# Conformer convolution on one core: shifted copies by way of DRAM in five transfers a tile, and layer-norm sums added on GpSimd about a provisional mean

## The chip, the cores and the metric

The program runs on one core of one Trainium2 chip. The metric is the device time of one launch in microseconds (us). PE is TensorE's matmul, PEld its weight load, DVE VectorE, ACT ScalarE, POOL GpSimd, SP SyncE, which issues nearly all transfers here; SPq is its DMA issue. Line numbers (L242) are those of the kernel before.

## The reference, cut to what matters

Two layers of a conformer step over 512 prompt tokens and 8 sample tokens, 1024 features wide. Layer 0 mixes with attention, layer 1 with this convolution module; each layer has two feed-forward halves and an embedding step around it.

```
def conv_module(h, buf, w_in, w_dw, b_dw, ln_g, ln_b, w_out):
    u = h @ w_in
    g = u[..., :D_MODEL] * jax.nn.sigmoid(u[..., D_MODEL:])
    xc = jnp.concatenate([buf.astype(g.dtype), g], axis=1)
    y = lax.conv_general_dilated(xc, w_dw[:, None, :], window_strides=(1,), padding='VALID', ...,
                                 feature_group_count=D_MODEL) + b_dw          # 31 taps, one filter a feature
    y = jax.nn.silu(layernorm(y, ln_g, ln_b))
    return y @ w_out, xc[:, -(CONV_WIDTH - 1):]
def layernorm(x, g, b):
    mu = jnp.mean(xf, axis=-1, keepdims=True)
    var = jnp.mean(jnp.square(xf - mu), axis=-1, keepdims=True)
    y = (xf - mu) * lax.rsqrt(var + LN_EPS) * g + b
```

## The kernel before, in words

Activations lie with features on the 128 partitions (eight feature tiles, k = 0 to 7) and the 520 tokens along the free axis, in PSUM as two halves of 260. Every large product is three matmuls: weights and activations are split into a high part and a rest (`w_hi`, `w_lo`, `h_hi`, `h_lo`), and `products` (L242) runs hi*hi, hi*lo and lo*hi. A weight slab of 128 x 1024 is fetched by SP into `w_raw` (`load_slab`, L221), split by ACT (L227) and DVE (L231), and used by PE. The order on each engine is the order in which the code is written; semaphores alone join the engines.

The stage that the change touches is the convolution of layer 1, in the functions `conv_sp`, `conv_pe`, `conv_act`, `conv_dve` and `conv_pool`. For each feature tile k:

- PE makes the two halves of `w_in` (`tile(k, 0)` and `tile(k, 1)`, 48 matmuls each). DVE brings them out of PSUM (`scaled`, L293), ACT takes the sigmoid (L1700), DVE multiplies them (`gated`, L1766) into `g_pad`, which holds 30 zeros ahead of 512 tokens in two buffers.
- Of the 31 taps, 28 go to PE. For these `g4` holds four copies of the tile, each shifted by j = 0 to 3 tokens, on 32 partitions per shift, with the features in four groups of 32. SP makes them in `shifted(k)` with 16 transfers from SBUF to SBUF (L1505), one for each shift and group. PE then runs `taps_pe(k)` (L1556): 28 matmuls (56 in the trace) with `diag4`, the taps spread over small diagonals, which POOL makes (L1847) from `tap4`, the taps in the same arrangement. `tap4` is filled by another 16 transfers (L1517) from `taps_j`.
- The last 3 taps are DVE's (`own_taps`, L1777 and L1781). `finish(k)` (L1789 to L1795) adds both parts into y. It runs one tile later than the tile's products.
- For the layer norm PE sums y over features by matmuls with ones (`ln_sum`, L1564), tile by tile, two tiles behind, into one PSUM slot. After the last tile DVE subtracts the mean from each of the eight tiles (L1823), ACT squares each (L1718), and PE sums each square with ones (L1602); ACT makes 1/sqrt (L1723, L1725); DVE scales (L1827), ACT applies Silu (L1728) and makes `c_hi`, DVE makes `c_lo` (L1834), and only then can the products with `w_out` begin (`conv_out_pe`).

PE's written order is tile(0,0), tile(0,1), tile(1,0), 16 transposes of the convolution's state, tile(1,1), taps 0, and from k = 2 on tile(k,0), tile(k,1), taps k-1, `ln_sum(k-2)`. After the loop come eight small transposes (L1594), `ln_sum(6)`, taps 7, `ln_sum(7)` and the sums of squares. SP's written order puts the transfers for `tap4` ahead of `shifted(0)`, and the slabs of tile b+3 ahead of `shifted(b+1)`.

Of the kernel before, what the change touches and what calls it, by code (L numbers as in the profile page):

```python
# [48 lines left out]
def build(nc, io):  # L49
# [4 lines left out]
    with ctx:  # L54
# [54 lines left out]
        conv_kept = (("g_last", [P, KD, PAD + NS], F32), ("y", [P, KD, T], F32), ("cv_tok", [PAD + NS, D], F32))  # L109
        g_last, y, cv_tok, ident4, taps_j, tap4, g_pad, g4, diag4, own_a, own_b, st_rows, st = phase_memory(  # L110
            *conv_kept, ("ident4", [P, Q], F32), ("taps_j", [P, 4, KD, GROUPS], F32), ("tap4", [P, 4, KD, GROUPS], F32),
            ("g_pad", [P, 2, PAD + TP], F32), ("g4", [P, 2, 4, GW], F32), ("diag4", [P, KD, 4, GROUPS, Q], F32),
# [372 lines left out]
        def load_sp(sp):  # L485
# [24 lines left out]
        def load_pool(pool):  # L510
# [979 lines left out]
        def conv_sp(sp):  # L1490
# [23 lines left out]
            sp.wait_ge(taps_j_ok, 1)  # L1514
            for j in range(4):
                for g in range(4):
                    sp.dma_start(tap4[j * Q:(j + 1) * Q, g, :, :], taps_j[g * Q:(g + 1) * Q, j, :, :]).then_inc(tap4_in, 16)  # L1517
            shifted(0)
# [17 lines left out]
        def conv_pe(pe):  # L1536
# [9 lines left out]
            def taps_pe(k):  # L1546

                pe.wait_ge(g4_in[k % 2], 256 * (k // 2 + 1))
                pe.wait_ge(diag4_ok, k + 1)
                if k < 2:  # L1550
                    pe.wait_ge(state_ok, 3)
                else:
                    pe.wait_ge(y_ok, k - 1)
                for i in range(GROUPS):
                    for g in range(4):
                        ins = pe.matmul(ps[g * Q:(g + 1) * Q, 3, k % 2, :], diag4[:, k, g, i, :],  # L1556
                                        g4[:, k % 2, g, 4 * i:4 * i + TP], start=i == 0, stop=i == GROUPS - 1)
                ins.then_inc(taps_mm, 1)

            def ln_sum(k):  # L1560

                pe.wait_ge(y_ok, k + 1)
                for b in range(2):
                    ins = pe.matmul(slot(2)[:, b, :], ones[:, :], y[:, k, b * HALF:(b + 1) * HALF],  # L1564
                                    start=k == 0, stop=k == KD - 1)
                return ins

# [27 lines left out]
            ins.then_inc(tail_mm, 1)  # L1595
            ln_sum(KD - 2)
            taps_pe(KD - 1)
            ln_sum(KD - 1).then_inc(ln_mm, 1)
            for k in range(KD):
                pe.wait_ge(ysq_ok, k + 1)  # L1600
                for b in range(2):
                    ins = pe.matmul(slot(1)[:, b, :], ones[:, :], square[:, k % 2, b * HALF:(b + 1) * HALF],  # L1602
                                    start=k == 0, stop=k == KD - 1)
                ins.then_inc(ln_mm, 1)

# [58 lines left out]
        def conv_out_dve(dve):  # L1664
# [22 lines left out]
            for m in range(6, KD):  # L1687
                split_lo(dve, n0 + m, m % 2)
                add(m - 2)
                x_post_dve(dve, CO, 1, 2, m - 2)  # L1690

        def conv_act(act, prev):
            n0 = C["slab"]
# [8 lines left out]
            for j in range(2):  # L1702
                split_hi(act, n0 + 2 + j, n0 // 2 + 1, j)
                if j == 0:
                    stat_act(act, C)
            sigmoid(0)
            for k in range(1, KD):
                if k < KD - 1:
                    for j in range(2):
                        split_hi(act, n0 + 2 * k + 2 + j, n0 // 2 + k + 1, j)  # L1710
                sigmoid(k)
            for j in range(2):
                split_hi(act, CO["slab"] + j, CO["slab"] // 2, j)
            for k in range(KD):
                act.wait_ge(yc_ok, k + 1)
                if k >= 2:
                    act.wait_ge(ln_mm, k)
                act.activation(square[:, k % 2, :], y[:, k, :], ACT.Square).then_inc(ysq_ok, 1)  # L1718
# [3 lines left out]
            act.wait_ge(ln_mm, KD + 1)  # L1722
            act.activation(halves(s_gate[:, :]), slot(1), ACT.Ln, scale=1.0 / D, bias=eps[:, 1:2]).then_inc(var_ok, 1)  # L1723
            act.wait_ge(var_ok, 1)
# [8 lines left out]
        def conv_dve(dve, prev_evac, prev_lo):  # L1733
# [69 lines left out]
            for k in range(1, KD):  # L1803
# [9 lines left out]
                if k == 1:  # L1813
                    state_sum()
                finish(k - 1)
            own_taps(KD - 1)
            finish(KD - 1)
            for j in range(2):
                split_lo(dve, CO["slab"] + j, j)
            for k in range(KD):  # L1820
                dve.wait_ge(ln_mm, 1)
                yk = halves(y[:, k, :])
                dve.scalar_tensor_tensor(yk, slot(2), 1.0 / D, yk, ALU.mult, ALU.subtract).then_inc(yc_ok, 1)  # L1823
            dve.wait_ge(var_ok, 2)
            for k in range(KD):
                dve.wait_ge(ysq_ok, k + 1)
                dve.scalar_tensor_tensor(y[:, k, :], y[:, k, :], -1.0, s_up[:, :], ALU.mult, ALU.mult).then_inc(yn_ok, 1)  # L1827
# [8 lines left out]
        def conv_pool(pool):  # L1836
            pool.tensor_copy(taps_j[:, :, :, :], taps[:, 0:TAPS_PE * KD].rearrange(
                "p (i j k) -> p j k i", i=GROUPS, j=4)).then_inc(taps_j_ok, 1)
            pool.wait_ge(state_ok, 3)
# [3 lines left out]

            pool.wait_ge(tap4_in, 256)
            pool.wait_ge(ident4_ok, 1)
            for k in range(KD):
                pool.tensor_tensor(diag4[:, k, :, :, :], ident4[:, :].unsqueeze(1).unsqueeze(1).broadcast_to([P, 4, GROUPS, Q]),  # L1847
                                   tap4[:, :, k, :].unsqueeze(3).broadcast_to([P, 4, GROUPS, Q]), ALU.mult).then_inc(diag4_ok, 1)


# [299 lines left out]
```

## Time and profile before

| | |
|---|---|
| median of 3 runs | 2306.94 us (2306.43 to 2313.22) |
| the profiled execution | 2307.65 us, its span 2305.8 us |
| PE busy | 2212.5 us, 96% of the span |
| DVE, ACT, POOL busy | 1086.1, 752.1 and 130.8 us |
| chain that ended last | PE 85%, of which L242 80% of the span; SPq 2% on L1505 |
| convolution stage | from about 1602 to 1800 us of the span |

The slice view (40 slices of 57.6 us) has PE at nine tenths or more nearly throughout; three of the four slices that hold the convolution have 7, 8 and 8. PE bounds the kernel, so what counts are the places where it stands still, and the work that it is given.

### The profile page before, as it was taken

The page shows a single profiled execution, that of the slowest core. Times are in us where ns is not written, and L with a number is a line of the kernel's source. Part 1 is how long each engine was busy: PE and PEld are TensorE (multiplying, and loading weights), DVE is VectorE, ACT ScalarE, POOL GpSimd, SP SyncE. Part 2 cuts the span into 40 slices and gives each one's busy share as a digit, 9 for nine tenths or more (in the row PEclk, how much of TensorE's full clock was granted, in tenths as well). Part 3 has the DMA queues.
Part 4 walks back from the last instruction along what each step waited for, and adds up shares of the span by engine and source line. Part 5 has one row for each costly group of instructions (what it writes and reads, how often), then busy time and mean ns, then how long its engine had stood idle before and what let it go on. Part 6 is the DMA issues. An engine that isn't in the chain of part 4 may idle for free.

```text
span 2305.8 us, 43575 instructions
## 1 busy us (share of the span) xinstructions
PE 2212.5 (96%) x18009; PEld 2111.0 (92%) x18009; DVE 1086.1 (47%) x1269; ACT 752.1 (33%) x1011; POOL 130.8 (6%) x101
## 2 busy tenths in 40 slices
PE   7999999979998999999999999999798899999998
PEld 7999999967777999999999999999575899999998
DVE  5444433378884444443354444433633444443344
ACT  4222222446663322222244222222111532222223
POOL 2000001010000100000010000001300100000100
PEclk9999999989998999999999999999898999999999
DMA  3333332435673333333232333323443233333322
GB/s 113 91 91 91 105 88 83 153 94 187 220 239 106 101 91 91 91 99 97 68 101 83 91 91 91 103 88 91 109 129 82 58 92 91 91 91 100 94 71 83
DMA packets 380347, 237.98 MB, mean 103 GB/s; under 512 B 10090, under 2 KB 363850, under 8 KB 380264
## 3 DMA queue, kind: packets, MB, share of 16 engines
q1 hardware_dynamic: 371560, 232.56, 33.9%
q10 hardware_dynamic: 8704, 4.26, 0.6%
q8 instruction: 59, 0.97, 0.2%
q14 instruction: 24, 0.20, 0.0%
HBM read 220.36 MB, written 7.53 MB: 99 GB/s over the span
## 4 chain that ended last, share of the span: by engine, by line
PE 85%; DVE 6%; issue 3%; SPq 2%; ACT 2%; DMA 1%; ACTq 0%; DVEq 0%
PE ps L242 80%; SPq L1505 2%; PE ps L1556 2%; DVE sg_m L1325 1%; DVE kc L1341 1%; DVE w_lo L231 1%; DVE sg_p L1332 1%; PE ps L1891 1%; ACT w_hi L227 0%; SPq L1517 0%; DVE h_lo L259 0%; PE ps L809 0%; DMA g<-g_pad 0%; DMA xs_tok<-in_x_sample 0%; PE ps L1602 0%
## 5 line engine op out<-in xcount | busy, mean ns | idle before, releaser
L242 PE MATMUL ps<-h_hi,w_hi 128*128 128x260 f32 x3712 | 757.9, 285 | 13.6 <-DVE w_lo L231 9.0
L242 PE MATMUL ps<-h_hi,w_lo 128*128 128x260 f32 x3712 | 749.8, 284 | 0.0
L242 PE MATMUL ps<-h_lo,w_hi 128*128 128x260 f32 x3712 | 748.6, 283 | 0.0
L227 ACT ACTIVATE w_hi<-w_raw 128x1024 fp32r<-128x1024 f32 (+1 forms) x314 | 353.9, 1127 | 1140.4 <-PE ps L242 1098.3
L242 PEld LDWEIGHTS ps<-h_hi,w_hi 128*128 128x128 f32 x3712 | 575.5, 189 | 22.3 <-DVE w_lo L231 10.9
L242 PEld LDWEIGHTS ps<-h_hi,w_lo 128*128 128x128 f32 x3712 | 574.0, 189 | 0.0
L242 PEld LDWEIGHTS ps<-h_lo,w_hi 128*128 128x128 f32 x3712 | 573.1, 189 | 0.0
L231 DVE TENSOR_TENSOR w_lo<-w_raw,w_hi 128x1024 fp32r<-128x1024 f32 (+1 forms) x316 | 420.0, 1329 | 270.4 <-ACT w_hi L227 270.0
L242 PE MATMUL ps<-a_hi,w_hi 128*128 128x260 f32 x1408 | 283.9, 283 | 0.0
L242 PE MATMUL ps<-a_hi,w_lo 128*128 128x260 f32 x1408 | 283.2, 282 | 0.0
L242 PE MATMUL ps<-a_lo,w_hi 128*128 128x260 f32 x1408 | 282.7, 282 | 0.0
L293 DVE TENSOR_TENSOR s_up<-ps,rms 128x520 f32<-128x520 f32 x108 | 75.6, 700 | 338.3 <-PE ps L242 332.1
L242 PEld LDWEIGHTS ps<-a_lo,w_hi 128*128 128x128 f32 x1408 | 217.3, 188 | 0.0
L242 PEld LDWEIGHTS ps<-a_hi,w_hi 128*128 128x128 f32 x1408 | 216.7, 188 | 0.0
L242 PEld LDWEIGHTS ps<-a_hi,w_lo 128*128 128x128 f32 x1408 | 216.6, 188 | 0.0
L293 DVE TENSOR_TENSOR s_gate<-ps,rms 128x520 f32<-128x520 f32 x116 | 81.2, 700 | 189.0 <-PE ps L242 149.3
L299 DVE SCALAR_TENSOR_TENSOR x<-ps,x 128x520 f32 (+1 forms) x42 | 29.4, 700 | 199.0 <-PE ps L242 199.0
L272 POOL TENSOR_TENSOR sumsq<-sumsq,square 128x520 f32<-128x520 f32 x56 | 87.4, 1561 | 480.4 <-ACT square L255 450.1
L317 ACT ACTIVATE a_hi<-s_prod 128x520 f32 (+1 forms) x88 | 56.2, 639 | 176.2 <-DVE s_prod L324 176.2
L326 DVE TENSOR_TENSOR a_lo<-s_prod,a_hi 128x520 f32 (+1 forms) x88 | 61.6, 700 | 80.7 <-ACT a_hi L317 80.7
L269 POOL COPY sumsq<-square 128x520 f32<-128x520 f32 x8 | 6.7, 840 | 1534.9 <-ACT square L255 1511.2
L259 DVE SCALAR_TENSOR_TENSOR h_lo<-x,gains,h_hi 128x520 fp32r<-128x520 f32 (+1 forms) x64 | 80.6, 1267 | 3.4 <-ACT h_hi L253 2.0
(215 smaller groups left out, 1562.4 us busy)
## 6 DMA issues: line engine op xcount, KB each, us to landing
w_raw<-in_ffn_wg SPq DMA_DIRECT2D x88, 512.0 KB, 3.8
w_raw<-in_ffn_wu SPq DMA_DIRECT2D x88, 512.0 KB, 3.8
w_raw<-in_ffn_wd SPq DMA_DIRECT2D x64, 704.0 KB, 4.4
kc<-in_cache_k SPq DMA_DIRECT2D x32, 512.0 KB, 5.5
vc<-in_cache_v SPq DMA_DIRECT2D x28, 512.0 KB, 5.9
w_raw<-in_attn_w_qkv SPq DMA_DIRECT2D x24, 512.0 KB, 4.5
g<-g_pad SPq DMA_DIRECT2D x128, 67.0 KB, 2.1
w_raw<-in_ple_w_gate SPq DMA_DIRECT2D x16, 512.0 KB, 3.7
```

What stands on the lines that cost most here:

```text
L227: act.activation(w_hi[:, j, 0:cols], w_raw[:, j, 0:cols], ACT.Copy).then_inc(slab_hi, 1)
L231: dve.tensor_tensor(w_lo[:, j, 0:cols], w_raw[:, j, 0:cols], w_hi[:, j, 0:cols].bitcast(F32), ALU.subtract).then_inc(slab_lo, 1)
L242: ins = pe.matmul(out[:, b_, :], a[:, j, w], b[:, k0 + k, b_ * HALF:(b_ + 1) * HALF], start=(first and k == kts[0] and n == 0), stop=(last ...
L259: dve.scalar_tensor_tensor(h_lo[:, ds(m, 1), :].rearrange("p a t -> p (a t)"), x[:, ds(m, 1), :].rearrange("p a t -> p (a t)"), gain_col(l ...
L272: pool.tensor_tensor(sumsq[:, :], sumsq[:, :], square[:, m2, :], ALU.add).then_inc(acc_ok, 1)
L293: dve.tensor_tensor(halves(out), slot(s), halves(rms[:, :]), ALU.mult).then_inc(evac, 1)
L299: dve.scalar_tensor_tensor(xm, slot(s), factor, xm, ALU.mult, ALU.add).then_inc(evac, 1)
L317: act.activation(a_hi[:, ds(f, 1), :].rearrange("p a t -> p (a t)"), s_prod[:, :], ACT.Copy).then_inc(a_hi_ok, 1)
L326: dve.tensor_tensor(a_lo[:, ds(f, 1), :].rearrange("p a t -> p (a t)"), s_prod[:, :], a_hi[:, ds(f, 1), :].rearrange("p a t -> p (a t)").b ...
L1325: ins = dve.tensor_tensor_scan(m, m, zero[:, :].broadcast_to([P, (i + 1) * P]), 1.0, ALU.mult, ALU.max)
L1505: sp.dma_start(g4[j * Q:(j + 1) * Q, k % 2, g, :], g_pad[g * Q:(g + 1) * Q, k % 2, j:j + GW]).then_inc(g4_in[k % 2], 16)
L1556: ins = pe.matmul(ps[g * Q:(g + 1) * Q, 3, k % 2, :], diag4[:, k, g, i, :], g4[:, k % 2, g, 4 * i:4 * i + TP], start=i == 0, stop=i == GRO ...
```

## The change

Four parts.

1. `shifted(k)`: one transfer writes `g_pad` to a DRAM buffer `g_rows` (128 rows of 542 values), SP waits until it has landed, and four transfers (one a shift, 32 partitions x 4 groups x 536 values) read it into `g4`. `gated(k)` now waits for the write of tile k-2 and no longer for its shifted copies.
2. `taps_j` is made by POOL at the start of the program, in memory of the loading phase, and written to a DRAM buffer `taps_rows` by SP; four transfers fill `tap4` from there, ahead of the state's load. POOL's part before `diag4` is now only the product for the state.
3. The sum of y is formed by POOL, tile by tile, in `y_sum` (the memory of `sumsq`), and PE sums it over features twice: after four tiles (`across`, within k = 5) and after eight. Twice the first sum over 1024 is `mean_4`, a provisional mean.
4. DVE takes each tile's deviation from `mean_4` (`deviation`), ACT squares it, POOL adds the squares in `d_sum` (the memory of `log_ms`); tiles 0 to 6 within the loop by the table `DEVS`, tile 7 at the end. PE sums `d_sum` once. The variance is that sum over 1024 less the square of (true mean - `mean_4`). The eight `ln_sum` and the eight sums of squares on PE are gone. DVE's two splits of the first `w_out` slabs now stand before `finish(7)`, and y is centred behind the sums.

```
-        g_last, y, cv_tok, ident4, taps_j, tap4, ... = phase_memory(
+        g_last, y, cv_tok, ident4, mean_4, tap4, ... = phase_memory(
...
+        taps_rows = nc.dram_tensor("taps_rows", (P, 4 * KD * GROUPS), F32, kind="Internal").ap()
+        g_rows = nc.dram_tensor("g_rows", (2, P, PAD + TP), F32, kind="Internal").ap()
+        y_sum, d_sum, dev = sumsq, log_ms, s_prod
...                                                     (load_sp, its end)
+            sp.wait_ge(taps_j_ok, 1)
+            sp.dma_start(taps_rows[:, :], taps_j[:, :, :, :].rearrange("p j k i -> p (j k i)")).then_inc(taps_rows_in, 16)
...                                                     (load_pool, its end; was the start of conv_pool)
+            pool.wait_ge(vec_ok, 2)
+            pool.tensor_copy(taps_j[:, :, :, :], taps[:, 0:TAPS_PE * KD].rearrange(
+                "p (i j k) -> p j k i", i=GROUPS, j=4)).then_inc(taps_j_ok, 1)
...                                                     (shifted, in conv_sp)
+                sp.dma_start(g_rows[k % 2], g_pad[:, k % 2, :]).then_inc(g_rows_in, 16)
+                sp.wait_ge(g_rows_in, 16 * k + 16)
                 for j in range(4):
-                    for g in range(4):
-                        sp.dma_start(g4[j * Q:(j + 1) * Q, k % 2, g, :],
-                                     g_pad[g * Q:(g + 1) * Q, k % 2, j:j + GW]).then_inc(g4_in[k % 2], 16)
+                    sp.dma_start(g4[j * Q:(j + 1) * Q, k % 2, :, :],
+                                 g_rows[k % 2].rearrange("(g c) t -> c g t", g=4)[:, :, j:j + GW]).then_inc(g4_in[k % 2], 16)
...                                                     (conv_sp; the tap4 loop after both(2) is gone)
+            sp.wait_ge(taps_rows_in, 16)
+            for j in range(4):
+                sp.dma_start(tap4[j * Q:(j + 1) * Q, :, :, :].rearrange("p g k i -> p g (k i)"),
+                             taps_rows.rearrange("(g c) (j r) -> j c g r", g=4, j=4)[j]).then_inc(tap4_in, 16)
...                                                     (conv_pe)
-            def ln_sum(k):
...
+            def across(s, src):
                 for b in range(2):
+                    ins = pe.matmul(slot(s)[:, b, :], ones[:, :], src[:, b * HALF:(b + 1) * HALF], start=True, stop=True)
+                ins.then_inc(ln_mm, 1)
...
                 tile(k, 1)
+                if k == 5:
+                    pe.wait_ge(y_sum_ok, 4)
+                    across(2, y_sum)
                 taps_pe(k - 1)
-                ln_sum(k - 2)
...
-            ln_sum(KD - 2)
             taps_pe(KD - 1)
-            ln_sum(KD - 1).then_inc(ln_mm, 1)
-            for k in range(KD):
-                pe.wait_ge(ysq_ok, k + 1)
...
+            pe.wait_ge(mean_4_ok, 1)
+            pe.wait_ge(y_sum_ok, KD)
+            across(2, y_sum)
+            pe.wait_ge(d_sum_ok, KD)
+            across(1, d_sum)
...
+        DEVS = {k: {5: (0, 1), 6: (2, 3, 4), 7: (5, 6)}.get(k, ()) for k in range(KD)}
...                                                     (conv_act)
+            def squared(k):
+                act.wait_ge(dev_ok, k + 1)
+                if k >= 2:
+                    act.wait_ge(d_sum_ok, k - 1)
+                act.activation(square[:, k % 2, :], dev[:, :], ACT.Square).then_inc(ysq_ok, 1)
...
+            act.wait_ge(off_ok, 1)
+            act.activation(s_act[:, :], dev[:, :], ACT.Square).then_inc(off_ok, 1)
+            act.wait_ge(off_ok, 3)
+            act.activation(s_gate[:, :], s_gate[:, :], ACT.Ln, bias=eps[:, 1:2]).then_inc(var_ok, 1)
...                                                     (conv_dve)
-                    dve.wait_ge(g4_in[k % 2], 256 * (k // 2))
+                    dve.wait_ge(g_rows_in, 16 * (k - 1))
...
+            def deviation(k):
+                dve.wait_ge(mean_4_ok, 1)
+                dve.wait_ge(y_ok, k + 1)
+                if k:
+                    dve.wait_ge(ysq_ok, k)
+                dve.tensor_tensor(dev[:, :], y[:, k, :], mean_4[:, :], ALU.subtract).then_inc(dev_ok, 1)
...
             own_taps(KD - 1)
-            finish(KD - 1)
             for j in range(2):
                 split_lo(dve, CO["slab"] + j, j)
+            finish(KD - 1)
+            deviation(KD - 1)
+            dve.wait_ge(ln_mm, 2)
+            dve.wait_ge(ysq_ok, KD)
+            dve.scalar_tensor_tensor(halves(dev[:, :]), slot(2), 1.0 / D, halves(mean_4[:, :]),
+                                     ALU.mult, ALU.subtract).then_inc(off_ok, 1)
...
+            centred(0)
+            centred(1)
+            dve.wait_ge(ln_mm, 3)
+            dve.wait_ge(off_ok, 2)
+            dve.scalar_tensor_tensor(halves(s_gate[:, :]), slot(1), 1.0 / D, halves(s_act[:, :]),
+                                     ALU.mult, ALU.subtract).then_inc(off_ok, 1)
+            for k in range(2, KD):
+                centred(k)
...                                                     (conv_sums_pool, new, run behind conv_pool)
+            for k in range(5):
+                add_y(k)
+            for k in range(5, KD):
+                for d in DEVS[k]:
+                    add_d(d)
+                add_y(k)
+            add_d(KD - 1)
```

`add_y(k)` waits for y of tile k and adds it to `y_sum` (the fifth also waits until PE has read the first sum); `add_d(k)` waits for the square and adds it to `d_sum`; the first of each is a copy.

**The order on SP**, from the last slabs ahead of the convolution to the shifted copies of tile 1. Before:

```order
L1511 DMA st_rows<-in_state_conv 120x2x1024
L221 DMA w_raw<-in_conv_w_in 128x8x128 x2
L1517 DMA tap<-taps_j 32x56 x16
L1505 DMA g<-g_pad 32x536 x16
L221 DMA w_raw<-in_conv_w_in 128x8x128 x2
L1525 DMA out_new_conv_sample<-st_rows 29x2x1024
L1505 DMA g<-g_pad 32x536 x16
```

Of the change, whose line numbers are its own:

```order
L1530 DMA tap<-taps_rows 32x4x56 x4
L1532 DMA st_rows<-in_state_conv 120x2x1024
L232 DMA w_raw<-in_conv_w_in 128x8x128 x2
L1519 DMA g_rows<-g_pad 128x542
L1522 DMA g<-g_rows 32x4x536 x4
L232 DMA w_raw<-in_conv_w_in 128x8x128 x2
L1542 DMA out_new_conv_sample<-st_rows 29x2x1024
L1519 DMA g_rows<-g_pad 128x542
L1522 DMA g<-g_rows 32x4x536 x4
```

Sixteen small transfers have gone from ahead of the first shifted copies, four stand ahead of the state's load, and each group of sixteen has become one and four.

**The order on DVE**, from the last of DVE's own taps on. Before:

```order
L1781 SCALAR_TENSOR_TENSOR own_a<-g_pad,taps,own_a 128x512
L1789 TENSOR_TENSOR own_b<-own_b,ps 128x512
L1792 SCALAR_TENSOR_TENSOR y<-g_last,taps,y 128x8
L1795 TENSOR_TENSOR y<-own_a,own_b 128x512
L231 TENSOR_TENSOR w_lo<-w_raw,w_hi 128x1024 x2
L1823 SCALAR_TENSOR_TENSOR y<-ps,y 128x520 x8
L1827 SCALAR_TENSOR_TENSOR y<-y,s_up 128x520 x2
```

Of the change (`s_prod` is the memory of `dev`, `mean` is `mean_4`):

```order
L1810 SCALAR_TENSOR_TENSOR own_a<-g_pad,taps,own_a 128x512
L242 TENSOR_TENSOR w_lo<-w_raw,w_hi 128x1024 x2
L1818 TENSOR_TENSOR own_b<-own_b,ps 128x512
L1821 SCALAR_TENSOR_TENSOR y<-g_last,taps,y 128x8
L1824 TENSOR_TENSOR y<-own_a,own_b 128x512
L1796 TENSOR_TENSOR s_prod<-y,mean 128x520
L1857 SCALAR_TENSOR_TENSOR s_prod<-ps,mean 128x520
L1864 SCALAR_TENSOR_TENSOR y<-ps,y 128x520 x2
L1870 SCALAR_TENSOR_TENSOR s_gate<-ps,s_act 128x520
L1864 SCALAR_TENSOR_TENSOR y<-ps,y 128x520 x6
L1877 SCALAR_TENSOR_TENSOR y<-y,s_up 128x520 x2
```

The two weight splits have moved ahead of the end of y, and three instructions have come in behind it.

**The order on POOL**, behind the state's product, of the change (before, only the product and the eight `diag` stood here):

```order
L1888 TENSOR_TENSOR st<-st,taps 128x1920
L1895 TENSOR_TENSOR diag<-ident,tap 128x896 x8
L1904 COPY sumsq<-y 128x520
L1909 TENSOR_TENSOR sumsq<-sumsq,y 128x520 x4
L1915 COPY log_ms<-square 128x520
L1918 TENSOR_TENSOR log_ms<-log_ms,square 128x520
L1909 TENSOR_TENSOR sumsq<-sumsq,y 128x520
L1918 TENSOR_TENSOR log_ms<-log_ms,square 128x520 x3
L1909 TENSOR_TENSOR sumsq<-sumsq,y 128x520
L1918 TENSOR_TENSOR log_ms<-log_ms,square 128x520 x2
```

One more addition of each kind follows. Sixteen instructions of 128 x 520 have come to POOL.

## Rows read from the trace of the kernel before

**Rows 1.** Waits between 1600 and 1900 us: in total, times, longest.

```profile
PE ps L1556 <- DMA g<-g_pad: 18.7, 4, 11.8
```

**Rows 2.** The chain that ended last, 1590 to 1880 us: start, duration, what.

```profile
1617.33 0.91 SPq L1517
...
1680.26 6.22 PE ps L1556 x56
...
1780.11 2.27 DVE w_lo L231 x2
...
1797.46 0.83 ACT y L1728
1798.31 0.65 ACT c_hi L1731
1798.98 0.71 DVE c_lo L1834
...
1799.83 54.61 PE ps L242 x432
```

**Rows 3.** PE in order of time, in brackets idle time ahead and its releaser.

```profile
1639.42 9.10 PE L1556 MATMUL ps<-g,diag 128*32 128x512 f32 x56 [11.76 <-DMA g<-g_pad]
...
1660.16 6.22 PE L1556 MATMUL ps<-g,diag 128*32 128x512 f32 x56
1666.30 1.14 PE L1564 MATMUL ps<-y,ones 128*128 128x260 f32 x4
...
1769.88 8.73 PE L1556 MATMUL ps<-g,diag 128*32 128x512 f32 x56 [4.74 <-DMA g<-g_pad]
```

**Rows 4.** Windows: engines' busy time, PEclk, DMA share, GB/s.

```profile
1636.00:1637.00 1.00, 0.00 (x0) 0.00 (x0) 1.00 (x2) 0.53 (x1) 1.00 (x1) 0.50 0.59 137
...
1772.00:1773.00 1.00, 1.00 (x8) 0.20 (x4) 0.00 (x0) 0.13 (x1) 0.00 (x0) 0.50 1.01 391
...
1799.83:1805.50 5.67, 5.67 (x26) 5.67 (x27) 5.17 (x9) 5.54 (x9) 0.00 (x0) 0.50 0.00 0
```

**Rows 5.** SP's issues in order of time, convolution stage.

```profile
1617.33 10.43 SPq L1517 DMA_DIRECT2D tap<-taps_j  x16
...
1758.32 10.02 SPq L1505 DMA_DIRECT2D g<-g_pad  x16
```

**Rows 6.** DMA issues by kind: count, KB each, median us to landing.

```profile
g<-g_pad SPq DMA_DIRECT2D x128, 67.0 KB, 2.1
...
out_y_prompt<-out_tok SPq DMA_DIRECT2D x8, 256.0 KB, 2.2
```

**Rows 7.** POOL: two rows in order of time, one group of the page.

```profile
1623.54 5.41 POOL L1840 TENSOR_TENSOR st<-st,taps 128x1920 f32<-128x1920 f32 x1 [16.61 <-DVE st L1748]
1628.96 16.48 POOL L1847 TENSOR_TENSOR diag<-ident,tap 128x896 f32<-128x896 f32 x8
...
L272 POOL TENSOR_TENSOR sumsq<-sumsq,square 128x520 f32<-128x520 f32 x56 | 87.4, 1561 | 480.4 <-ACT square L255 450.1
```

**Rows 8.** DVE in order of time.

```profile
1617.62 0.69 DVE L1766 TENSOR_TENSOR g_pad<-s_up,s_act 128x512 f32<-128x512 f32 x1 [0.72 <-ACT s_act L1700]
...
1623.99 6.05 DVE L231 TENSOR_TENSOR w_lo<-w_raw,w_hi 128x1024 fp32r<-128x1024 f32 x1
...
1638.38 2.18 DVE L1766 TENSOR_TENSOR g_pad<-s_up,s_act 128x512 f32<-128x512 f32 x1
...
1750.50 0.70 DVE L293 TENSOR_TENSOR s_up<-ps,rms 128x520 f32<-128x520 f32 x1 [5.41 <-PE ps L242]
...
1782.30 4.94 DVE L1823 SCALAR_TENSOR_TENSOR y<-ps,y 128x520 f32<-128x520 f32 x8
...
1796.18 1.31 DVE L1827 SCALAR_TENSOR_TENSOR y<-y,s_up 128x520 f32<-128x520 f32 x2 [8.95 <-ACT s_up L1725]
```

**Rows 9.** The start of the program, POOL and SP in order of time.

```profile
14.61 0.70 POOL L269 COPY sumsq<-square 128x520 f32<-128x520 f32 x1 [9.98 <-ACT square L255]
...
21.98 0.42 SPq L221 DMA_DIRECT2D w_raw<-in_ffn_wg  x1
```

More of the change, by code:

```diff
@@ L109, in build @@
         conv_kept = (("g_last", [P, KD, PAD + NS], F32), ("y", [P, KD, T], F32), ("cv_tok", [PAD + NS, D], F32))
-        g_last, y, cv_tok, ident4, taps_j, tap4, g_pad, g4, diag4, own_a, own_b, st_rows, st = phase_memory(
-            *conv_kept, ("ident4", [P, Q], F32), ("taps_j", [P, 4, KD, GROUPS], F32), ("tap4", [P, 4, KD, GROUPS], F32),
+        g_last, y, cv_tok, ident4, mean_4, tap4, g_pad, g4, diag4, own_a, own_b, st_rows, st = phase_memory(
+            *conv_kept, ("ident4", [P, Q], F32), ("mean_4", [P, T], F32), ("tap4", [P, 4, KD, GROUPS], F32),
             ("g_pad", [P, 2, PAD + TP], F32), ("g4", [P, 2, 4, GW], F32), ("diag4", [P, KD, 4, GROUPS, Q], F32),
@@ L172, in build @@
         taps_j_ok = sem("taps_j_ok")
+        taps_rows_in = sem("taps_rows_in")
+        g_rows_in = sem("g_rows_in")
+        y_sum_ok = sem("y_sum_ok")
+        d_sum_ok = sem("d_sum_ok")
+        dev_ok = sem("dev_ok")
+        mean_4_ok = sem("mean_4_ok")
+        off_ok = sem("off_ok")
         tap4_in = sem("tap4_in")
@@ L1513, in conv_sp @@
             both(2)
[L1514 to L1517, printed above, removed]
             shifted(0)
@@ L1546, in taps_pe @@
             def taps_pe(k):
-                pe.wait_ge(g4_in[k % 2], 256 * (k // 2 + 1))
+                pe.wait_ge(g4_in[k % 2], 64 * (k // 2 + 1))
                 pe.wait_ge(diag4_ok, k + 1)
@@ L1595, in conv_pe @@
             ins.then_inc(tail_mm, 1)
-            ln_sum(KD - 2)
             taps_pe(KD - 1)
-            ln_sum(KD - 1).then_inc(ln_mm, 1)
-            for k in range(KD):
-                pe.wait_ge(ysq_ok, k + 1)
[L1601 to L1604, printed above, removed]
+            pe.wait_ge(mean_4_ok, 1)
[3 more added lines that the diff above has]
+            across(1, d_sum)
         CO = at["mixout", 1]
@@ L1711, in conv_act @@
                 sigmoid(k)
+                for d in DEVS[k]:
+                    squared(d)
             for j in range(2):
                 split_hi(act, CO["slab"] + j, CO["slab"] // 2, j)
[L1714 to L1718, printed above, removed]
+            squared(KD - 1)
             act.wait_ge(tail_mm, 1)
@@ L1815, in conv_dve, with centred @@
                 finish(k - 1)
+                if k == 5:
+                    dve.wait_ge(ln_mm, 1)
+                    dve.tensor_scalar(halves(mean_4[:, :]), slot(2), 2.0 / D, None, ALU.mult).then_inc(mean_4_ok, 1)
+                for d in DEVS[k]:
+                    deviation(d)
             own_taps(KD - 1)
-            finish(KD - 1)
             for j in range(2):
                 split_lo(dve, CO["slab"] + j, j)
-            for k in range(KD):
-                dve.wait_ge(ln_mm, 1)
+            finish(KD - 1)
[4 more added lines that the diff above has]
+                                     ALU.mult, ALU.subtract).then_inc(off_ok, 1)
+            def centred(k):
+                dve.wait_ge(dev_ok, k + 1)
+                dve.wait_ge(y_sum_ok, k + 1)
                 yk = halves(y[:, k, :])
                 dve.scalar_tensor_tensor(yk, slot(2), 1.0 / D, yk, ALU.mult, ALU.subtract).then_inc(yc_ok, 1)
+            centred(0)
[6 more added lines that the diff above has]
+                centred(k)
             dve.wait_ge(var_ok, 2)
             for k in range(KD):
-                dve.wait_ge(ysq_ok, k + 1)
+                dve.wait_ge(yc_ok, k + 1)
                 dve.scalar_tensor_tensor(y[:, k, :], y[:, k, :], -1.0, s_up[:, :], ALU.mult, ALU.mult).then_inc(yn_ok, 1)
@@ L1842, in conv_pool @@
                                    [P, KD, NS, PAD]), ALU.mult).then_inc(st_prod, 1)
-            pool.wait_ge(tap4_in, 256)
+            pool.wait_ge(tap4_in, 64)
             pool.wait_ge(ident4_ok, 1)
@@ L1848, in conv_pool, with conv_sums_pool, add_y, add_d @@
                                    tap4[:, :, k, :].unsqueeze(3).broadcast_to([P, 4, GROUPS, Q]), ALU.mult).then_inc(diag4_ok, 1)
+        def conv_sums_pool(pool):
+            def add_y(k):
+                pool.wait_ge(y_ok, k + 1)
+                if k == 0:
+                    pool.wait_ge(stat_mm, C["norm"] + 1)
+                    pool.tensor_copy(y_sum[:, :], y[:, 0, :]).then_inc(y_sum_ok, 1)
+                else:
+                    pool.wait_ge(y_sum_ok, k)
+                    if k == 4:
+                        pool.wait_ge(ln_mm, 1)
+                    pool.tensor_tensor(y_sum[:, :], y_sum[:, :], y[:, k, :], ALU.add).then_inc(y_sum_ok, 1)
+            def add_d(k):
+                pool.wait_ge(ysq_ok, k + 1)
+                if k == 0:
+                    pool.wait_ge(rms_ok, C["norm"] + 1)
+                    pool.tensor_copy(d_sum[:, :], square[:, 0, :]).then_inc(d_sum_ok, 1)
+                else:
+                    pool.wait_ge(d_sum_ok, k)
+                    pool.tensor_tensor(d_sum[:, :], d_sum[:, :], square[:, k % 2, :], ALU.add).then_inc(d_sum_ok, 1)
+            for k in range(5):
+                add_y(k)
+            for k in range(5, KD):
+                for d in DEVS[k]:
+                    add_d(d)
+                add_y(k)
+            add_d(KD - 1)
         y_mm = sem("y_mm")
@@ L2059, in _ @@
                 (attn_pool, conv_pool)[layer](pool)
+                if layer == 1:
+                    conv_sums_pool(pool)
                 add_squares_pool(pool, at["mixout", layer])
```

13 lines of the change are left out of this document (3 added, 10 removed).

## The prediction

> **What bounds the kernel now.** The page's busy shares come first: PE is busy 96% of the span and the chain runs 85% through it, so only time in which PE stands still in the convolution stage, or work that it no longer gets, can move the end. The waits view of that stage names the largest stall: PE waited four times for the shifted copies, 18.7 us in all, 11.8 of them once [rows 1]. PE in order of time places them [rows 3]: 11.76 us ahead of taps 0 and 4.74 ahead of taps 7, so 2.2 us are left for the other two. The reader should then look at what PE does next. Taps 0 and taps 7 took 9.10 and 8.73 us, taps 1, without a gap, 6.22 [rows 3], and taps 2, behind one of the small gaps, 6.22 too [rows 2]: after both long gaps the granted clock was at its lower level, as it also was when the products with `w_out` began (0.50 in the 5.67 us from 1799.83) [rows 4]. The chain [rows 2] shows what lay under the first gap: not the copy itself, but SP, busy from 1617.33 with the 16 transfers for `tap4` (10.43 us) before it came to the copies of tile 0 [rows 5]. It shows a third place: y of the last tile is written at 1780.11, and the products with `w_out` begin at 1799.83 [rows 2]. These 19.7 us are the layer norm, one pass behind another.
>
> The sum is made against the profiled execution, 2307.65 us, which lies 0.7 above the median 2306.94; the terms are taken over unchanged. About 0.3% (7 us) is what a measurement can tell from no change here.
>
> **Price of a transfer.** A small copy of 67 KB lands 2.1 us after its issue [rows 6]. While only such copies ran, the DMA engines moved 137 GB/s at a busy share of 0.59 [rows 4], 232 at full share. So of the 2.1 us some 0.3 is the data and 1.8 is fixed. The write of `g_rows` has 277 KB: 1.8 + 1.2 = 3.0 us by this, and 2.2 by the nearest row, the output's 256 KB to DRAM [rows 6]; I take 2.2 and keep 3.0. The four reads have 1.1 MB together: 1.8 + 4.7 = 6.5 us from first issue to last landing. If they ran at the fastest rate seen (391 GB/s, `w_out` slabs over 128 partitions) [rows 4] it would be 4.6. I take 6.5, since the reads fill the same 32 partitions with rows of the same length as the copies that gave 232. So the chain from `g_pad` to taps is 2.2 + 6.5 and 0.2 for two handovers, 8.9 us, against some 10.0 of issuing and 2.1 of landing now [rows 5, 6].
>
> The Trainium skill (SBUF — State Buffer, section "Door 1: The DMA port swizzle") says that 32 partitions reach only half of the ports and end at about 218 GB/s. That speaks against the fast end, and the rate scaled from the row, 232, is near it. By the fit of the page DMA: Bandwidth & Descriptors (section "Anatomy of one DMA"), 2.0 us and bytes at 436 GB/s, the whole chain would be 7.4 us, and the sum below would gain 1.5 us more.
>
> **1. First gap.** With `tap4` filled long before, SP comes to tile 0 as soon as `g_pad` is there, at 1618.3 [rows 8]. A weight slab is in flight ahead of the write (a delay of up to 2 us); the copies land by 1618.4 + 3.0 + 2 + 6.5 = 1629.9 at the latest. Next to be late is POOL: the state's product ends at 1628.95 and the first of eight `diag` takes 16.48 / 8 = 2.06 us [rows 7]. Taps 0 can start at 1631.2 in place of 1639.42: **-8.2 us**. PE still stands for 3.5 us, so I leave taps 0 at the 9.1 us it took. It couldn't use a faster one: `g_pad` of tile 1 is written slowly, at 1640.5 (2.18 us beside POOL) [rows 8], its copies land at about 1640.6 + 2.5 (slab and state rows ahead in the queue) + 2.2 + 6.5 = 1651.8, and PE arrives there at 1631.2 + 9.1 + 11.6 (the two halves between taps 0 and taps 1 [rows 3]) = 1651.9. A gain in clock would be lost in that wait; a slower chain costs here at once. Bounds 5 and 10.
>
> **2. PE's work inside the loop.** Each `ln_sum` is 1.14 us as a group, 1.07 apart [rows 3]. Five (tiles 0 to 4) stand where PE is the bound and go; those of tiles 5 and 6 stand in the gap ahead of taps 7 and give nothing; one `across` comes in at k = 5. 5 x 1.07 - 1.07 = **-4.3 us**. The sum it waits for was finished by POOL some 8 us before.
>
> **3. The two small waits** of 2.2 us together [rows 1, 3]. The copies are wanted some 16 us after `g_pad` and were late because their issue crawled behind slabs; the new chain needs 8.9 and up to 4 for the slab ahead of it: **-2.2 us**, bounds 0 and 2.2.
>
> **4. Last gap.** `g_pad` of tile 7 is there when SP issues at 1758.32 [rows 5]. Taps 7 can start at 1758.4 + 8.9 = 1767.3, against 1769.88: **-2.6 us**. PE has lost two `ln_sum` in this gap, so it stands for 4.74 + 2 x 1.07 - 2.6 = 4.3 us. The gap of 4.74 cost the clock, the two small ones did not [rows 2, 3]; 4.3 is nearer to the former, so taps 7 stays at 8.7. Bounds 0 and, with fast reads and the clock held, 4.5 + 2.5 = 7.
>
> **5. The tail.** From y's last write to the first `w_out` product, the longest path is now: POOL's addition of tile 7, 1.56 [rows 7]; `across`, 1.1 [rows 3]; on DVE the offset, 0.6, eight centrings, 4.94 [rows 8], the variance, 0.7, and one scaling, 0.65 [rows 8]; then Silu 0.83, `c_hi` 0.65, `c_lo` 0.71 [rows 2]; handovers 0.6. Sum 12.3 us against 19.7: **-7.4 us**. The other branch (deviation, square, POOL's second addition, `across`, variance, Ln, Exp) ends near 6.9 us, while DVE still centres until 9.3, so it is covered by 2.4 us. The lower clock at the start of the `w_out` products [rows 4] stays, since PE stands for over 7 us there. The splits of the `w_out` slabs now stand ahead of `finish(7)`; their slabs are issued at about 1764 and are split by 1773, taps 7 ends at 1776. Bounds 4 and 9.
>
> **6. What costs nothing.** POOL's copy of the taps runs at about 13.5 us, before its first addition at 14.61, and SP's write then stands in a wait that lasts until 21.98 [rows 9]. Of the new work, 7 deviations on DVE and 7 squares on ACT lie in the loop, where DVE stands idle 5.4 us before each tile's first half is done [rows 8]; the densest place (tile 6: `finish`, three deviations that wait for squares) needs about 5.0. Without that cover each us over it delays the bringing out of a half, which matters only after another 5 us or so.
>
> Sum: 8.2 + 4.3 + 2.2 + 2.6 + 7.4 = 24.7 us. 2307.65 - 24.7 = 2283.0, and 2282.2 on the median.
>
> **Rivals.**
> (A) *Reads at full rate.* If the reads from DRAM move as the slabs do, taps 7 starts at 1765.4, the gap is 2.4 us, and the clock may hold: 1.9 + 2.5 more, 2278. For it: 391 GB/s was seen. Against: not into 32 partitions. Chance 0.2.
> (B) *DVE and POOL in each other's way.* The split that began at 1623.99 took 6.05 us, against 1.14 for one of the two at 1780.11, and ended 1.1 us after POOL's product did [rows 2, 7, 8]. So DVE stood until POOL was through. In the tail, the deviation and POOL's addition start together; 0.7 us more if DVE goes first. In tile 6 and 7, ten additions of 1.56 us stand beside DVE's deviations, own taps and splits; if every second of them blocks DVE, `g_pad` of tile 7 comes about 3 us late and `finish(7)` 1 to 2 us: about 5 us back, 2287. Against: all of it together fits into the tile's 18 us. Chance 0.15. The Trainium skill (SBUF — State Buffer, section "Who interferes with whom") has the rule: an instruction of VectorE with two SBUF inputs and one of GpSimd that reads SBUF exclude each other for their whole length; by that rule this is the full block that the row shows, and the centrings, which read PSUM, are free of it.
> (C) *The way through DRAM is the new bound.* SP itself waits for the write, with the reads and the slabs of the next tiles queued behind it. In the loop taps k is wanted about 15.5 us after `g_pad`(k), and 3 to 4 of these go to the slab ahead, so it decides once write and reads take over 12 us. For a result slower than before by 7 us, the six tiles in the loop and the last must give back 32 us: 2.7 us of gap and 2.6 of slow clock at each of six, that is write and reads in 15 us, 2314 or more. For it: a write is now ahead of every read and no row here shows that pair back to back. Against: 2.2 us for 256 KB to DRAM. Chance 0.03.
> (D) *The gain is mostly given back*: chain at 12 us, first gap only moved to taps 1 with a second cold start, tail held by the statistics: 2300 to 2310. Chance 0.05.
>
> **Numbers.** My forecast 0.57, A 0.2, B 0.15, D 0.05, C 0.03. The bounds of the five terms, not all at one end, give 15 to 33 us off; with A and B inside, the range is 2274 to 2292. Faster by over 0.3% is everything but C and about half of D, 0.94; within 0.3%, 0.04; slower 0.02.
>
> **What would show it.** Taps 0 starting near 1631 with POOL's `diag` as releaser, and a wait of under 1 us ahead of taps 1; no wait of PE for the copies of tiles 2 to 6; taps 7 about 11 us after the end of `tile(7,1)` (1756.1 before, 1740 or so now) and still near 8.7 us; 12 us between y's last write and the first `w_out` product, with DVE busy in most of it. I am wrong on the transfers if PE waits for copies within the loop, on the tail if DVE's scaling waits for Exp, and on POOL if DVE's own taps or splits take over 2 us there.

## The result and the profile after

| | before | changed |
|---|---|---|
| median of 13 runs each | 2308.3 us | 2304.4 us |
| ratio, 95% interval | | 0.9979 (0.9971 to 0.9988) |
| profiled span | 2305.8 us | 2305.1 us |
| stage, from the norm's sum (L278, now L289) to the first `w_out` product | 191.97 us | 187.66 us |

The change gains about 4 us; 24.7 had been forecast. The two profiled spans differ by only 0.7 us because the changed kernel's stage happened to begin 3.7 us later in its run. Single runs of either kernel scatter by 9 to 10 us from the lowest to the highest, so I compare stages within a trace and medians of runs. One run of one experiment (the transfers alone, 3088.81 us at a granted clock of 0.65 against 0.98 in its others) was in a slower state and is left out of that experiment's numbers. Line numbers below are those of the kernel shown.

The waits view of the changed kernel, 1590 to 1900 us (total, times, longest), answers to [rows 1]:

```profile
PE ps L1573 <- DMA g<-g_rows: 17.5, 3, 7.7
```

The same view for SP:

```profile
SPq L1522 <- DMA g_rows<-g_pad: 57.9, 8, 12.1
```

PE still waits 17.5 us for copies, nearly as long as before. SP waits 7.2 us on average for a write that I had priced at 2.2, because it now has to see each write land before it may issue the reads. PE in order of time, answering to [rows 3]:

```profile
1635.44 8.72 PE L1573 MATMUL ps<-g,diag 128*32 128x512 f32 x56 [4.07 <-issue]
...
1663.57 8.32 PE L1573 MATMUL ps<-g,diag 128*32 128x512 f32 x56 [7.70 <-DMA g<-g_rows]
1683.69 6.22 PE L1573 MATMUL ps<-g,diag 128*32 128x512 f32 x56
1706.78 8.89 PE L1573 MATMUL ps<-g,diag 128*32 128x512 f32 x56 [5.14 <-DMA g<-g_rows]
...
1775.72 8.56 PE L1573 MATMUL ps<-g,diag 128*32 128x512 f32 x56 [4.61 <-DMA g<-g_rows]
1787.28 2.05 PE L1579 MATMUL ps<-sumsq,ones 128*128 128x260 f32 x4 [3.01 <-POOL sumsq L1909]
```

The first gap did shrink, from 11.76 to 4.07 us. But two new ones have opened, ahead of taps 1 and taps 3, and both were followed by the low clock (8.3 and 8.9 us against 6.22). SP's issues show what stood behind them, in answer to [rows 5]:

```profile
1642.67 0.44 SPq L1542 DMA_DIRECT2D out_new_conv_sample<-st_rows  x1
1644.35 0.34 SPq L1519 DMA_DIRECT2D g_rows<-g_pad  x1
1656.25 1.75 SPq L1522 DMA_DIRECT2D g<-g_rows  x4
...
1730.42 0.41 SPq L1519 DMA_DIRECT2D g_rows<-g_pad  x1
1734.75 1.75 SPq L1522 DMA_DIRECT2D g<-g_rows  x4
...
1749.14 0.34 SPq L1519 DMA_DIRECT2D g_rows<-g_pad  x1
1751.56 1.73 SPq L1522 DMA_DIRECT2D g<-g_rows  x4
```

The time from a write to the reads behind it is the write's landing. It was 11.9 us where a store of the sample's state rows (L1542) had been issued just ahead (tile 1), 4.3 behind two weight slabs (tile 5), and 2.4 with nothing ahead (tile 6). All four tiles with a store ahead (1 to 4) read 11.9 to 13.3. The windows of the first of them (columns as in [rows 4]):

```profile
1645.00:1646.00 1.00, 1.00 (x11) 1.00 (x10) 1.00 (x2) 0.00 (x0) 1.00 (x2) 1.00 0.97 342
1647.00:1656.00 9.00, 8.86 (x74) 8.65 (x73) 7.07 (x11) 1.10 (x2) 2.85 (x3) 1.00 0.07 27
1659.00:1663.00 4.00, 0.00 (x0) 0.00 (x0) 0.00 (x0) 0.00 (x0) 0.00 (x0) 0.75 1.07 203
```

The slabs are through by 1646. Then, for nine microseconds, the DMA share is 0.07, about one engine of sixteen, and 27 GB/s flow: 9 x 27 is 243 KB, close to the 232 KB of the store. So I read it like this: the store has 29 rows and runs on one DMA engine, a sixteenth of the write goes to that engine too, and SP waits for it. The experiments below test this reading. The last row shows the reads with slabs among them: all engines busy, 203 GB/s.

### The profile page after: what moved, and what is told of

The parts are those of the page before. It is cut to its first block, busy times and chain, and to the rows that moved or that the text cites. A ratio compares the mean times of both kernels' runs of the same rounds, so it can differ in the third digit from the quotient of the medians.

```text
span 2305.1 us, 43436 instructions
## 1 busy us (share of the span) xinstructions
PE 2207.5 (96%) x17957; PEld 2105.6 (91%) x17957; DVE 1099.3 (48%) x1280; ACT 752.8 (33%) x1012; POOL 152.4 (7%) x117
## 4 chain that ended last, share of the span: by engine, by line
PE 83%; DVE 7%; issue 4%; DMA 3%; ACT 2%; POOL 1%; ACTq 0%; SPq 0%; DVEq 0%; POOLq 0%
PE ps L253 79%; DVE sg_m L1341 1%; DMA g_rows<-g_pad 1%; DVE kc L1357 1%; PE ps L1573 1%; DVE w_lo L242 1%; PE ps L1969 1%; DVE sg_p L1348 1%; DVE zs L1362 1%; DMA g<-g_rows 1%; POOL log_ms L1918 0%; PE ps L825 0%; DMA w_raw<-in_attn_w_qkv 0%; ACT w_hi L238 0%; DVE h_lo L270 0%
```

## The experiments

Theory S: the store's single engine holds up the write. Rival W: a write to DRAM is slow under the slabs' traffic. Rival P: the loss lies in the sums, where POOL holds up DVE.

### Without the stores

```
-                sp.dma_start(out[b, 0:PAD - 1, :, :], rows).then_inc(conv_out, 16)
...
-            sp.wait_ge(conv_out, 96)
+            sp.wait_ge(conv_out, 32)
```

> The changed kernel with the four stores of 29 kept state rows left out (those rows of new_conv_sample are not written). Theory S: each store of 232 KB runs on one of the 16 DMA engines (share 0.06 to 0.07 for some 9 us behind the slabs), and the write of g_rows, one sixteenth of which goes to the same engine, lands 12 us after its issue in place of 2 to 3. Then all eight writes land in 2 to 5 us, PE's waits ahead of taps 1 and taps 3 (7.7 and 5.1 us, and 4.8 of low clock behind them) go, and the time is 2287, 17 to 18 under the change. Rival W: a write to DRAM under the slabs' traffic is slow by itself. Then the four writes of tiles 1 to 4 still land in 8 us or more and the time stays at 2300 to 2305.

2284.5 us, ratio 0.9900 (0.9882 to 0.9918). The eight writes land in 2.2 to 4.9 us with the slabs still ahead of them, and the waits ahead of taps 1 and 3 are gone. W falls.

### The stores moved behind the copies

```
                 both(b + 3)
-                sp.dma_start(out[b, 0:PAD - 1, :, :], rows).then_inc(conv_out, 16)
                 shifted(b + 1)
+                sp.dma_start(out[b, 0:PAD - 1, :, :], rows).then_inc(conv_out, 16)
```

> The changed kernel with each of the four stores issued behind the copies of its tile instead of ahead of them. Theory S: the write of g_rows finds the engine free, since the store before it ended 5 us or more earlier, and lands in 2 to 5 us; but the slabs of the next tile now follow the store, and the second of them may land up to 4 us later, which DVE and PE have slack for. 2288, up to 2293 if slabs are late. Rival W: no better than the change, 2300 to 2305.

2289.1 us, 0.9917 (0.9900 to 0.9933). Exchanging two lines brings 15 us. The store now slows the slabs instead: their median landing rises from 4.0 to 5.9 us, and small waits of 1.5, 0.3 and 1.2 us remain ahead of taps 3, 4 and 5. One part of the expectation failed: the writes of tiles 2 to 5 still took 6.8 to 9.7 us, 3 to 6 of them in being issued, and not 2 to 5. They were issued behind the slowed slabs; PE had time to spare for most of it.

### One direct copy in DRAM

```
+            kept = (PAD - 1) * D // 16
+            sp.dma_start(io["new_conv_sample"][0].rearrange("b w f -> b (w f)")[:, 0:16 * kept].rearrange("b (c r) -> c b r", c=16),
+                         io["state_conv"][0].rearrange("b w f -> b (w f)")[:, D:D + 16 * kept].rearrange(
+                             "b (c r) -> c b r", c=16)).then_inc(conv_out, 16)
```

at the head of `conv_tail_sp`, in place of the four stores.

> The changed kernel with the kept state rows copied once from input to output in DRAM, in 16 equal pieces a sample, behind the slabs of w_out, in place of the four stores. Theory S: as without stores, 2287; the 0.95 MB take 4 to 6 us on all engines while nothing is waited for. Rival W: 2300 to 2305.

2285.4 us, 0.9902 (0.9885 to 0.9918), with every output written. SP and PE of this kernel, tile 1 and the taps:

```profile
1641.83 0.34 SPq L1519 DMA_DIRECT2D g_rows<-g_pad  x1
1644.26 1.75 SPq L1522 DMA_DIRECT2D g<-g_rows  x4
```
```profile
1632.92 7.85 PE L1576 MATMUL ps<-g,diag 128*32 128x512 f32 x56 [4.08 <-issue]
1652.41 6.21 PE L1576 MATMUL ps<-g,diag 128*32 128x512 f32 x56
...
1754.42 8.53 PE L1576 MATMUL ps<-g,diag 128*32 128x512 f32 x56 [4.58 <-DMA g<-g_rows]
```

The write of tile 1 lands in 2.4 us, and taps 1 starts without a wait. The stage takes 168.9 us, from 1609.06 to 1777.94, 23.1 under before. The reads of tile 6, behind which nothing was issued for 12 us, in a window of the same kernel (columns as in [rows 4]):

```profile
1732.00:1736.00 4.00, 4.00 (x36) 4.00 (x35) 2.39 (x4) 1.28 (x2) 3.44 (x2) 1.00 1.06 229
```

All engines are busy, and they move 229 GB/s.

### The kernel before without the stores, and with the direct copy

The same two edits in the kernel before.

> The kernel before with the four stores left out (those rows of new_conv_sample are not written). Theory S: in the kernel before, the single-engine store runs beside 14 us of issuing of sixteen copies and is over when the last copy is issued, so without it SP's issue of the copies shrinks from 14 to 11 or 10 us and only the two small waits of PE (2.2 us together) and little else go: 2304 to 2308, a change of 0 to 4. Rival: the stores hold up both kernels alike, and this one gains 10 us or more too.

> The kernel before with the direct store in place of the four. As without stores (2302.1 measured), 2301 to 2304: the share of the whole gain that needs nothing of the change.

2302.1 us, 0.9974 (0.9962 to 0.9985), and 2304.3 us, 0.9979 (0.9970 to 0.9987). The first gained 6.5 us and not 0 to 4: SP's sixteen issues shrank from 14 us and more to 10 or 11, as expected, but two small waits of PE went and taps 0 and taps 7, behind the long gaps, came out 0.8 and 0.9 us shorter. So by the medians the stores cost the kernel before 4 to 7 us and the changed kernel 19 to 20 (18 by the ratios). On equal terms, with the direct copy in both, the change is worth 2304.3 - 2285.4 = 18.9 us, and the stages of the two traces differ by as much (187.8 against 168.9).

### Each half alone

First parts 3 and 4 of the change with the old copies, then parts 1 and 2 with the old layer norm.

> The kernel before with only parts 3 and 4 of the change: sums on GpSimd, the provisional mean, sixteen copies a tile as before. From the changed kernel's tail (13.4 us from y's last write to the first w_out product, against 19.7) and 4.3 us of PE work, theory S expects 10 to 11 us under before: 2298. Rival P: the additions on POOL hold up DVE in the loop and eat that gain; then it is 2304 or more and DVE's own taps and splits take over 2 us beside POOL's additions.

> The kernel before with only parts 1 and 2: the way through DRAM, taps ready early, layer norm as before, stores ahead of the copies. Theory S: the first gap shrinks by 7 to 8 us, but waits of 5 to 8 us with the lower clock behind them open at two of tiles 1 to 4 (17 us in all), so this half alone is slower than before by 4 to 8 us: 2313 to 2317. Rival P (the loss lies in the sums): it is faster than before by 12 us or more.

2299.4 us, 0.9958 (0.9944 to 0.9971), and 2312.5 us, 1.0016 (1.0006 to 1.0027). The product of the ratios, 0.9974, lies within the interval of the change's 0.9979. The way through DRAM, as it was put in, made the kernel slower; the sums carried the whole gain, and P falls.

### 28 rows and one row

```
-                sp.dma_start(out[b, 0:PAD - 1, :, :], rows).then_inc(conv_out, 16)
+                sp.dma_start(out[b, 0:PAD - 2, :, :], rows[0:PAD - 2]).then_inc(conv_out, 16)
+                sp.dma_start(out[b, PAD - 2:PAD - 1, :, :], rows[PAD - 2:PAD - 1]).then_inc(conv_out, 16)
...
-            sp.wait_ge(conv_out, 96)
+            sp.wait_ge(conv_out, 160)
```

> The changed kernel with each store of 29 rows split into one of 28 rows and one of a single row, still from SBUF and still ahead of the write. If the number 29 is what puts the store on one engine, the 28 rows spread over fourteen: the share of 0.06 for 9 us is gone, the writes of g_rows land in 3 to 5 us and the time is 2286 to 2290. If a store of rows of 4 KB from 29 partitions is slow for another reason, the writes still take 8 us or more and it stays at 2300 to 2305.

2287.2 us, 0.9902 (0.9886 to 0.9917). SP at tile 1 of this kernel:

```profile
1640.05 0.58 SPq L1542 DMA_DIRECT2D out_new_conv_sample<-st_rows  x1
1640.67 0.73 SPq L1543 DMA_DIRECT2D out_new_conv_sample<-st_rows  x1
1641.72 0.36 SPq L1519 DMA_DIRECT2D g_rows<-g_pad  x1
1645.15 1.74 SPq L1522 DMA_DIRECT2D g<-g_rows  x4
```

The same bytes, from the same place, at the same point of the queue, and the write behind them lands in 3.4 us instead of 11.9 (3.6 to 4.1 at tiles 2 to 4, instead of 12.5 to 13.3). It is the number 29 that costs.

The Trainium skill (DMA: Bandwidth & Descriptors, section "Why a DMA increments its semaphore by 16 and not by 1") has the rule: the number of engines is the largest up to 16 that divides the outermost size of both sides, so 29 rows get one engine and 28 get fourteen. The share of 0.07 and this run agree with the first; the fourteen were not counted in any trace. It stood there to be applied before the prediction.

### The stores from ACT's queue

The four stores issued in `conv_act` by ACT, one in each of k = 1 to 4, ahead of the sigmoid.

> The changed kernel with the same four stores of 29 rows issued by ACT instead of SP, one a tile, each behind ACT's weight splits. The store still runs on one DMA engine. If that engine takes its queues in turn, the write's share on it (17 KB) lands within 3 to 5 us and the time is 2286 to 2292. If the engine works through the store first, whichever queue it came from, the writes still take 8 us or more and it stays near 2300.

2294.6 us, 0.9943 (0.9923 to 0.9962), between the two expected ranges. SP at tile 2 of this kernel:

```profile
1651.86 0.81 SPq L1519 DMA_DIRECT2D g_rows<-g_pad  x1
1662.54 3.42 SPq L1522 DMA_DIRECT2D g<-g_rows  x4
```

Writes still took 10.7, 12.3 and 10.7 us at tiles 2 to 4; that of tile 1 was free (2.5 us), and ACT had issued its store 13 us earlier, against 3 us at the others. While the write of tile 2 was awaited, the DMA share was again 0.06 (from 1658 to 1661 us). So issuing the store from a second queue did not part it from the write. Whether the engine takes its queues in turn, with the slabs' share in the way, or finishes the store first, wasn't told apart.

### Two versions beyond the direct copy

In the first, the copies of tile 7 are again SBUF to SBUF, shifts 0 and 1 issued by SP, 2 and 3 by ACT. In the second, POOL makes the diagonals of tiles 0 to 3 ahead of the state's product. The third has both.

> The kernel with the direct store (2285), the last tile's copies made SBUF to SBUF again, eight issued by SP and eight by ACT. Issue of eight at 0.63 us is 5.0, landing 2.1, so taps 7 starts about 7.2 us after g_pad in place of 9.6: 2.4 us gained, and if PE's gap of 2.2 in place of 4.6 us leaves the clock up, 2.5 more. 2283, or 2280 with the clock held. Rival: two queues share the same engines and issue no faster together, 12 us, and it is 2287 or more.

> The kernel with the direct store (2285), POOL making the diagonals of tiles 0 to 3 before the state's product instead of behind it. Taps 0 then waits for the copies of tile 0, about 3 us sooner than for the first diagonal, so PE's gap of 4.1 us shrinks to about 1 and the low clock in taps 0 (7.9 us against 6.2) may go: 2 to 5 us gained, 2281 to 2283, if the copies of tile 1 come sooner too, since POOL's block ends 8 us sooner and DVE writes g_pad of tile 1 faster. Rival: POOL's four diagonals now block DVE while it prepares tile 0 and tile 1, g_pad of tile 0 comes 2 us or more later, and nothing is gained: 2284 to 2288.

> The direct store, the diagonals of tiles 0 to 3 first, and the last tile's copies from two queues, all three. If the gains add: 2278 to 2281, the best so far; if the diagonals bring nothing, as the two-queue kernel, 2281 to 2284.

2282.8 us, 0.9885 (0.9870 to 0.9900); 2285.4 us, 0.9896 (0.9879 to 0.9912); 2283.5 us, 0.9884 (0.9866 to 0.9902). So the diagonals first brought nothing, neither alone nor with the two queues. The stage of the first took 165.5 us (1604.28 to 1769.81) against 168.9 of the direct copy. With two queues the wait ahead of taps 7 fell as expected from 4.6 to 2.0 us. In the trace of the first version the low clock came all the same; in that of the third, behind the same wait, it did not:

```profile
1746.93 7.91 PE L1586 MATMUL ps<-g,diag 128*32 128x512 f32 x56 [2.04 <-DMA g<-g_pad]
```
```profile
1754.92 6.21 PE L1586 MATMUL ps<-g,diag 128*32 128x512 f32 x56 [2.05 <-DMA g<-g_pad]
```

So a gap of 2 us does not settle the clock by itself. Waits of 2.6 and 2.7 us in the traces of the two halves (ahead of taps 2 and of taps 7) were followed by 6.2 us too, one of 2.4 with the stores on ACT's queue by 7.9.

With the diagonals first, the wait ahead of taps 0 fell from 4.1 to 1.1 us and taps 0 ran at the high clock (6.21 us), but the time did not move. The chain of that kernel:

```profile
1639.58 4.36 DMA g_rows<-g_pad
...
1645.28 5.99 DMA g<-g_rows
...
1651.30 7.91 PE ps L1576 x56
```

PE came to taps 1 early and waited there 4.2 us for its copies, with the low clock behind the wait. The medians 2282.8 and 2283.5 lie under the direct copy's 2285.4, but the intervals overlap, so the two queues' 2 to 3 us are likely and not shown. All of these beat both kernels.

## Why the prediction was wrong

- **First gap** (-8.2). Right: 11.76 to 4.07 us, 7.7. POOL's first diagonal was what came late next: it took 2.68 us and not 2.06 and ended at 1635.3, and taps 0 began at 1635.44. The profile names no releaser there, but the gap shrank when the diagonals were made first. The further claim, that a gain in clock or in this gap would be lost in the wait for tile 1's copies, is what the run with the diagonals first showed.
- **PE's work in the loop** (-4.3). Somewhat too large. With the direct copy a tile takes 17.88 us (taps 1 to taps 2), against 18.71 in the kernel before without stores. A sum's group was worth 0.83 us and not 1.07, the rest overlaps its neighbours: -3.3 for five less one.
- **The small waits** (-2.2). **The step that failed.** "The new chain needs 8.9 and up to 4 for the slab ahead of it" allowed for the slab and not for the store, which stood in the same order of SP that the sum was made from. At tile 1 the state rows were named, but priced together with the slab at 2.5 us. The write took 11.9 to 13.3 us, taken at 2.2 from the row of the output's 256 KB, which doesn't show what stood ahead of it. In place of -2.2 there came 12.8 us of waits ahead of taps 1 and 3 and 4.8 of low clock. These 17.6 us, and 0.9 at taps 0, are nearly all of the 18.8 by which the stage of the change (187.66) exceeds that of the direct copy (168.9). Tiles 2 and 4 escaped, since PE, held up one tile earlier, came to them late.
- **Last gap** (-2.6). Nearly right: from the first issue to taps 7 it took 11.6 us before and 9.6 after, so -2.0. Of the changed kernel's 9.6, 7.3 us (1768.44 to 1775.72) lie between the first read's issue and taps 7, priced at 6.5; the rate itself was nearly as scaled (229 GB/s against 232, in the window of the direct copy), so rival A's reads at full rate did not come. The 7.4 us that the prediction worked out for the whole chain from the fit of the Trainium skill (DMA: Bandwidth & Descriptors, section "Anatomy of one DMA") is further off the 9.6; the page gives that fit for transfers issued by GpSimd, and SP issues these. Low clock behind it as expected (8.56 us). Whether a gap of 2.4 us would have kept the clock stays open: of two traces with 2.0 us there, one kept it and one did not.
- **The tail** (-7.4). 13.5 us from y's last write to the `w_out` products, so -6.2. DVE of the changed kernel there, answering to [rows 8]:

```profile
1785.09 0.69 DVE L1824 TENSOR_TENSOR y<-own_a,own_b 128x512 f32<-128x512 f32 x1
1785.87 1.82 DVE L1796 TENSOR_TENSOR s_prod<-y,mean 128x520 f32<-128x520 f32 x1
1789.37 0.70 DVE L1857 SCALAR_TENSOR_TENSOR s_prod<-ps,mean 128x520 f32<-128x520 f32 x1 [1.68 <-PE ps L1579]
...
1791.92 0.70 DVE L1870 SCALAR_TENSOR_TENSOR s_gate<-ps,s_act 128x520 f32<-128x520 f32 x1 [0.63 <-PE ps L1579]
1792.53 3.72 DVE L1864 SCALAR_TENSOR_TENSOR y<-ps,y 128x520 f32<-128x520 f32 x6
1796.17 1.30 DVE L1877 SCALAR_TENSOR_TENSOR y<-y,s_up 128x520 f32<-128x520 f32 x2
```

  The path is nearly the one foretold, centring to the end with the scaling straight behind it. Of the missing 1.2 us, 0.95 are PE's `across`, 2.05 us at the low clock (its row is above) where I had put 1.1. Another 0.6 is a wait that the sum put at nothing: the variance stands between the second and the third centring, and DVE waited there 0.63 us for the second `across`. POOL's addition, 1.28 us instead of 1.56, gave 0.3 back. The deviation took 1.82 us against 0.69 beside POOL's addition (rival B's mechanism). It lies on the way to the second `across`, for which PE waited 0.44 us, so by my estimate it cost at most that.
- **What costs nothing.** Right: the additions in the loop delayed no tile (17.88 us a tile with the direct copy). DVE's own taps of tile 7 took 1.5 us instead of 0.5 beside POOL, with room to spare.
- **The rivals.** C had the right mechanism, SP's wait with the reads behind it and the write as the long leg, and even its threshold of 12 us for write and reads. It was given 0.03, priced as a slowness of all tiles, and "a write is now ahead of every read and no row here shows that pair" was taken as a reason for doubt and not as a gap in the sum. D, at 0.05, had the time (2300 to 2310) and the picture of the first gap: 7.7 us of it came back as a wait ahead of taps 1, with a second stretch of low clock. But its chain of 12 us was too short (11.9 and 7.3, 19.2 us at tile 1), it named no cause for it, and the tail was not held by the statistics beyond the 0.6 us.

Without the stores the sum stands, term by term as the traces of the direct copy and of the kernel before give it: 7.7 + 1.2 (taps 0, 9.10 to 7.85) + 3.3 + 2.2 + 2.0 + 0.2 (taps 7) + 6.2 = 22.8 us, against 23.1 in the stage and 24.7 forecast.

## What to carry to other kernels

When a change puts a wait for a transfer's landing into a queue, price everything that was issued just ahead of it, not the transfer alone: sixteen copies that nobody waited for one by one had covered a slow store, and one write with a wait behind it laid it bare. Count the rows of each transfer's outer side; one of 29 rows ran at 27 GB/s on one engine, 28 and 1 did not. Where two halves of a change are independent, time them apart: here one gained 9.5 us and the other lost 4.

## What the runs showed that was not expected

- A store of 232 KB with 29 rows held 1 of 16 DMA engines for 9 us and raised the landing of a 271 KB write from 2.4 us (3.4 to 4.1 behind slabs and a split store) to 11.9 to 13.3. Issued from another engine's queue it still made it 10.7 to 12.3.
- In the kernel before the same stores cost 4 to 7 us, spread over slower issue of the small copies.
- PE's clock went either way behind waits of 2.0 to 2.7 us: 7.9 us for the taps after 2.04 and 2.35, 6.2 after 2.05, 2.62 and 2.67. In the traces here, gaps of 4.0 to 11.9 us ahead of taps were all followed by the low clock (7.6 to 9.1 us), gaps of 0.3 to 1.5 by none.
